# Adding the down projection's partial sums with a ScalarE copy and an accumulating DMA

## The reference, cut to what matters

```
h = rms_norm(x, pre_mlp_g)                         # x: 256 x 2048
m = jnp.square(jax.nn.relu(h @ w_up)) @ w_down     # w_up 2048 x 8192, w_down 8192 x 2048
x = x + rms_norm(m, post_mlp_g)
```

## Time and profile before

| what | value |
|---|---|
| time, two runs | 1110.64 and 1111.97 us, median 1111.31 us |
| profiled execution: span from its first to its last instruction | 1107.5 us |
| what lies around the span, by the faster run and by the median | 3.1 and 3.8 us |
| PE busy | 1091.9 us, 99% of the span |
| DVE, ACT, POOL busy | 666.2, 511.5, 98.3 us |
| DMA | 205.29 MB, mean 185 GB/s |

### The profile page before, as it was taken

The page is one execution under the profiler, slowest core; times in us unless marked ns, Lnnn a source line. Parts: engine busy times, 40 slices in busy tenths (PEclk is TensorE's granted clock), DMA queues, the critical chain, the costliest instruction groups (busy, mean ns, idle before and its releaser), DMA issues.

```text
span 1107.5 us, 13660 instructions
## 1 busy us (share of the span) xinstructions
PE 1091.9 (99%) x5034; PEld 906.2 (82%) x5034; DVE 666.2 (60%) x706; ACT 511.5 (46%) x653; POOL 98.3 (9%) x108
## 2 busy tenths in 40 slices
PE   8999999999999999999999999999999999999996
PEld 7888888887888778888888888888888888888884
DVE  5445564657985675565565655656556556565566
ACT  5564444544544464444444444444444444444443
POOL 0010120120000350000000000000000000000004
PEclk9999999999999999999999999999999999999998
DMA  9475454464755556565665655656656556566552
GB/s 330 159 227 158 155 176 138 152 196 138 274 190 191 157 185 190 189 191 160 214 190 186 197 178 192 195 159 210 189 184 200 179 189 195 166 202 193 190 172 76
DMA packets 104048, 205.29 MB, mean 185 GB/s; under 512 B 3536, under 2 KB 9552, under 8 KB 103504
## 3 DMA queue, kind: packets, MB, share of 16 engines
q1 hardware_dynamic: 104016, 204.86, 57.7%
HBM read 202.74 MB, written 2.10 MB: 185 GB/s over the span
## 4 chain that ended last, share of the span: by engine, by line
PE 95%; DVE 2%; ACT 1%; POOL 1%; issue 1%; DMA 0%; SPq 0%; DVEq 0%; POOLq 0%; ACTq 0%
PE ps L566 30%; PE ps L568 30%; PE ps L567 30%; PE ps L574 3%; DVE w_lo L1113 1%; PE ps L763 1%; PE ps L761 1%; DMA x_in<-in_x 0%; PE ps L811 0%; DVE xT_lo L1310 0%; ACT a_sb L1075 0%; ACT u_sb L939 0%; DVE acc L1339 0%; DVE x_res L1155 0%; DVE acc L1330 0%
## 5 line engine op out<-in xcount | busy, mean ns | idle before, releaser
L1113 DVE TENSOR_TENSOR w_lo<-raw,w_hi 128x1024 fp32r<-128x1024 f32 (+1 forms) x384 | 472.2, 1237 | 389.5 <-ACT w_hi L860 389.1
L860 ACT ACTIVATE w_hi<-raw 128x1024 fp32r<-128x1024 f32 (+1 forms) x384 | 398.1, 1039 | 492.7 <-PE ps L568 487.7
L566 PE MATMUL ps<-w_hi,xT_hi 128*128 128x512 f32 (+1 forms) x800 | 315.8, 395 | 1.9 <-DVE xT_lo L1125 0.7
L568 PE MATMUL ps<-w_lo,xT_hi 128*128 128x512 f32 (+1 forms) x800 | 310.0, 387 | 0.0
L567 PE MATMUL ps<-w_hi,xT_lo 128*128 128x512 f32 (+1 forms) x800 | 309.5, 387 | 0.0
L566 PE MATMUL ps<-w_hi,yT_hi 128*128 128x512 f32 x672 | 263.1, 392 | 0.0
L568 PE MATMUL ps<-w_lo,yT_hi 128*128 128x512 f32 x672 | 261.7, 389 | 0.0
L567 PE MATMUL ps<-w_hi,yT_lo 128*128 128x512 f32 x672 | 261.5, 389 | 0.0
L566 PEld LDWEIGHTS ps<-w_hi,xT_hi 128*128 128x128 f32 x800 | 150.5, 188 | 34.3 <-issue 5.6
L568 PEld LDWEIGHTS ps<-w_lo,xT_hi 128*128 128x128 f32 x800 | 150.4, 188 | 30.7
L567 PEld LDWEIGHTS ps<-w_hi,xT_lo 128*128 128x128 f32 x800 | 150.7, 188 | 27.9
(11 more groups left out here) (143 smaller groups left out, 459.8 us busy)
## 6 DMA issues: line engine op xcount, KB each, us to landing
raw<-in_w_up SPq DMA_DIRECT2D x64, 1024.0 KB, 5.3
raw<-in_w_down SPq DMA_DIRECT2D x64, 1024.0 KB, 5.0
raw<-in_w_in SPq DMA_DIRECT2D x31, 1024.0 KB, 5.2
raw<-in_w_o SPq DMA_DIRECT2D x16, 1024.0 KB, 5.1
raw<-in_w_uq SPq DMA_DIRECT2D x8, 576.0 KB, 4.0
raw<-in_w_ukv SPq DMA_DIRECT2D x4, 1024.0 KB, 5.0
raw<-in_w_in SPq DMA_DIRECT2D x4, 640.0 KB, 4.1
x_res<-in_x SPq DMA_DIRECT2D x1, 2048.0 KB, 9.2
```

The costliest lines, as they stand in the source:

```text
L566: nc.tensor.matmul(dst, x_hi, hi, start=first, stop=False)
L568: mm = nc.tensor.matmul(dst, x_hi, lo, start=False, stop=last)
L860: nc.scalar.activation(w_hi[:, slot, 0:size], raw[:, raw_slot, first:first + size], ACT.Copy).then_inc(hi_ready, 1)
L1113: nc.vector.tensor_tensor(w_lo[:, slot, 0:size], raw[:, raw_slot, first:first + size], f32(w_hi[:, slot, 0:size]), ALU.subtract).then_inc( ...
```

## The change

`add_down` leaves DVE. In its place ACT copies the finished PSUM pair into a new SBUF buffer `stage`, which has two places (quads even and odd), and POOL issues a DMA that adds that place to the columns of `acc` (`accum_op=ALU.add`). This holds for the 62 adds of a whole quad; the four block adds of `m_add` (1330) stay on DVE. Three semaphores take the place of `acc_added`: `acc_staged` (a copy is done, and PE may reuse the banks), `acc_landed[0]` and `acc_landed[1]` (a DMA of an even or odd quad has landed, 16 each), `acc_zeroed` (POOL's own memsets).

```diff
+            def stage_down(i, done, copies, landed):
+                act.wait_ge(half_used, done)
+                if landed is not None:
+                    act.wait_ge(acc_landed[i % 2], landed)
+                bank = 4 + 2 * (i % 2)
+                nc.scalar.activation(stage[:, i % 2], ps[:, bank:bank + 2], ACT.Copy).then_inc(acc_staged, 1)
...
+                elif what == "add":
+                    stage_down(a % 4, 2 * b + 2, a, 16 * (a // 2) if a >= 2 else None)
                 elif what == "m_square":
-                    act.wait_ge(acc_added, 4 * FF_STRIPS + a - 1)
+                    act.wait_ge(acc_landed[a], 16 * ((4 * (FF_STRIPS - 1) + a) // 2 + 1))
...
+                    if i >= 8 and i % 2:
+                        q = (i - 9) // 2
+                        stage_down(q, base + (i + 1), None, 32 * (j - 1) + 16 * (q // 2))
...
-            def add_down(i, done, added):
-                dve.wait_ge(half_used, done)
-                dve.wait_ge(acc_added, added)
-                m = acc[:, :, i * W:(i + 1) * W]
-                bank = 4 + 2 * (i % 2)
-                nc.vector.tensor_tensor(m, m, ps[:, bank:bank + 2], ALU.add).then_inc(acc_added, 1)
...
                     if i == 0:
                         dve.wait_ge(g_mlp_landed, 16)
-                        dve.wait_ge(acc_added, 4 * FF_STRIPS)
+                        for i_last in range(2):
+                            dve.wait_ge(acc_landed[i_last], 16 * (2 * FF_STRIPS - 1))
...
+            def add_down(i, copies):
+                pool.wait_ge(acc_staged, copies)
+                cols = slice(i * W, (i + 1) * W)
+                nc.gpsimd.dma_start(acc[:, :, cols], stage[:, i % 2], accum_op=ALU.add).then_inc(acc_landed[i % 2], 16)
...
-            with pool.Fori(LOOP.start, LOOP.stop) as j:
+            for j in LOOP:
                 square(j)
+                for q in range(4):
+                    add_down(q, (j - 1) * 4 + (q + 1))
```

More of the change, by code:

```diff
@@ L334, in hybrid_block @@
         gained = tensor(ctx, "gained", [P, TB, W])
+        stage = tensor(ctx, "stage", [P, 2, TB, W])
         ps = ctx.enter_context(nc.psum_tensor("ps", [P, 8, W], F32))
@@ L383, in hybrid_block @@
         aT_filled, aT_hi_ready, aT_lo_ready = sem("aT_filled"), sem("aT_hi_ready"), sem("aT_lo_ready")
-        acc_added = sem("acc_added")
+        acc_zeroed, acc_staged = sem("acc_zeroed"), sem("acc_staged")
+        acc_landed = [sem("acc_landed0"), sem("acc_landed1")]
         m_gained_pool = sem("m_gained_pool")
@@ L663, in stream @@
                         pe.wait_ge(aT_lo_ready, z["j"] + 1)
-                        pe.wait_ge(acc_added, 4 * z["j"] + z["q"] + 1)
+                        if 4 * z["j"] + z["q"] >= 2:
+                            pe.wait_ge(acc_staged, 4 * z["j"] + z["q"] - 1)
                         if z["j"] == 0:
@@ L694, in down_quad @@
             def down_quad(i, half, added):
-                pe.wait_ge(acc_added, added)
+                pe.wait_ge(acc_staged, added)
                 for k in range(4):
@@ L845, in _ @@
                 for i in range(4):
-                    down_quad(i, base + (8 + 2 * i), (j - 1) * 4 + (i + 1))
+                    down_quad(i, base + (8 + 2 * i), (j - 1) * 4 + (i - 1))
                 hidden_transposes(j)
@@ L1316, in step @@
                     hidden_lo(a, b)
-                elif what == "add":
-                    add_down(a % 4, 2 * b + 2, a + 2)
                 elif what.startswith("m_add"):
@@ L1355, in _ @@
                 for i in range(16):
-                    if i >= 8 and i % 2:
-                        add_down((i - 9) // 2, base + (i + 1), (j - 1) * 4 + ((i - 9) // 2 + 2))
                     split_lo(i % AHEAD, (i + AHEAD) // 2 % RAW, (i % 2) * 2 * W, 2 * W,
@@ L1482, in step @@
                     for tb in range(TB):
-                        nc.gpsimd.memset(acc[:, tb], 0.0).then_inc(acc_added, 1)
+                        nc.gpsimd.memset(acc[:, tb], 0.0).then_inc(acc_zeroed, 1)
+                    pool.wait_ge(acc_zeroed, TB)
                 elif what == "x2" and a >= X2_DVE:
@@ L1498, in step @@
                     square(a)
+                elif what == "add":
+                    add_down(a % 4, a + 1)
                 elif what == "m_square":
```

## The result

| | before | changed |
|---|---|---|
| time, two runs each | median 1111.31 us | 1117.72 and 1116.85, median 1117.28 us |
| ratio, 95% interval | | 1.0068, 1.0051 to 1.0084 |
| span of the profiled execution | 1107.5 us | 1115.8 us |
| busy DVE, ACT, POOL | 666.2, 511.5, 98.3 us | 596.2, 568.1, 172.5 us |

The time rose by 6.0 us, the span by 8.3 us; the forecast was +9.05. The changed kernel run again later, beside the kernel before on one chip, gave 1118.38 us against 1109.80 us, ratio 1.0080 (1.0066 to 1.0093).

A forecast was written before the change was run, and what follows sets the result against it. PE was taken to bound the loop, other engines' order the end. No loop cost; the end's sum, 2 D - 2.95 us, with D = 6.0 gives +9.05 us: span 1116.55, time 1120.4 us, range 1114 to 1130.5.

The forecast's parts named there:

- D: Time from a copy's end to its DMA's landing, POOL's issue included; estimated 6.0 us, bounds 3.2 and 11.1.
- Loop at no cost: In the strips, ACT copies, POOL issues and DMA traffic were to be hidden behind dense PE: cost 0.
- Copy 1.10 us: ACT's copy of a 128x1024 PSUM pair, taken as 1.10 us, four per strip.
- the slow DMAs: Rival: loop unharmed, D between 8 and 11.1 at the end, +13 to +19 us, 1124.4 to 1130.5; chance 0.13.
- Landing of quad 0 at 1087.46: At the end, strip 15: copy starts 1080.36, ends 1081.46, and its DMA lands at 1087.46.
- Landing of quad 1 at 1097.40: At the end: POOL, free at 1091.40 after its multiplies, issues quad 1's DMA, which lands at 1097.40.
- DVE's first block add waits for both DMAs: +8.40 us: At the end: DVE's first block add starts at 1097.40 instead of 1089.00.
- PE's stall of 2.4 us, at no cost: At the end: quad 3's second half is split late, moving PE's last matmul to about 1099, before DVE wants it.
- Span +9.05: Sum at the end: +8.40 us on DVE's block add and +0.65 us on ACT's squares, span 1116.55.
- the forecast's own case: D between 4.5 and 8, giving 1117.4 to 1124.4 us; chance 0.55.
- the quick DMA: Rival: D between 3.2 and 4.5 at the end, +3.4 to +6 us, 1114.7 to 1117.4; chance 0.20.
- The full engines: Rival: accumulating DMAs fill the 16 engines, loop weight loads come late; over 2% from 5.2 us per DMA; chance 0.11.

The follow-up runs named there:

- copies alone: The changed kernel without the 62 DMAs and the waits for them, ScalarE's copies kept, whole-quad adding left out: 1110.45 us, ratio 1.0001.
- sixty DMAs: The changed kernel with strip 15's two adds back on VectorE from PSUM, the 60 others still copies and accumulating DMAs: 1110.03 us, ratio 1.0001.
- with two DMAs: The changed kernel with a second accumulating DMA of the same staged copy into a spare buffer behind each of the 62: 1126.13 us, ratio 1.0152.
- with three: The kernel with two accumulating DMAs per add, plus a third of the same copy into a buffer no longer used: 1264.77 us, ratio 1.1387.
- The relaxed kernel: The changed kernel, but VectorE's first block add waits only for the DMAs up to strip 14: 1118.25 us, ratio 1.0072.
- a move of one line: The changed kernel with squares and multiplies of columns 0 moved behind quad 1's copy and DMA: 1113.88 us, ratio 1.0038.

## Why the prediction was right

The mechanism and the place were right, and each step can be held against the traces. The size of one term, D, was hit partly by luck.

- *Loop at no cost.* Shown: transposes 0.17 us apart after 14 strips, copies alone 1.0001, sixty DMAs 1.0001. The cover held with room: landings in the changed kernel came 8.5 us after the issue in the median and 11.2 at most (0.3 us more from the copy's end), under the 14.5 us from the copy's end at which I expected PE to stall. That threshold was reckoned too low: with two DMAs the last landing came up to 15.3 us after its issue and 16.3 after the copy, and PE was still dense; with three the median was 18.4 from the issue, and PE stalled.
- *Copy 1.10 us.* 1.03.
- *D = 6.0 for quad 0.* From the end of the copy, 1081.92, to the landing, 1087.95: 6.03, made of 1.04 before POOL's issue starts (0.30 in the loop) and 4.99 from issue to landing. The parts are not those of my sum. I added 1.0 for POOL's issue to a row of 5.0 that counts from the start of the issue; the measured 4.99 holds POOL's issue of 1.19 already. What filled the sum up to 6.03 was a delay before the issue that I had not in it: the total of D is right by luck in this part. Both ends of my range were far off, so the slow DMAs fall as well; the 1024 KB row was the right neighbour, and a plain DMA of 512 KB would have taken 3.12 us.
- *Landing of quad 0 at 1087.46.* 1087.95, since the copy began 0.53 us later: 0.17 of shift, and the rest a wait for the DMA of strip 14 that stood on the same place and had run beside other transfers.
- *Landing of quad 1 at 1097.40.* 1096.83. Here the term was too large: the copy had long ended when POOL came free, and from POOL's issue it is 4.96, not 6.0. The 1.0 too much outweighs the 0.5 us by which the first landing was late.
- *"DVE's first block add waits for both DMAs: +8.40 us"* puts the shift on the wrong wait. The relaxed kernel shows that. Between landing and end the chain goes over ACT's squares of columns 1 and then POOL's multiplies of 2.96 us, which hold POOL's first step of the reciprocal root. The shift is the same since all of them wait for the one landing; from the start of the block add to the end of the chain it took 15.0 us against the 15.3 of the sum. No run takes POOL's multiplies out of the way, so that they and not ACT's square of the block set the end is read from the chain only.
- *PE's stall of 2.4 us, at no cost.* Two gaps of 1.70 and 1.10 us in front of quad 3. Only the second waits for the split that I named; the first waits for the copy of quad 1, which I had not in the sum. The last matmul ended at 1100.15 instead of 1096.65, before VectorE's last block add at 1106.10. Harmless, as said.
- *Span +9.05.* +8.13 behind the loop, +8.3 in all; by the ratios +7.3 to +9.3 us in time. The missing 0.9 us is 0.6 of the second landing and 0.3 behind the block add. The first two runs (1117.28 us) lie just under the forecast's own case of 1117.4 to 1124.4, the later ones (1118.38) in it.

Of the rivals, the quick DMA (D of 3.2 to 4.5) was what a plain one does, 3.12 us from its issue; the price of adding excluded it, which was argued beforehand and is now measured. The Trainium skill's rule that an add in the DMA runs at half the rate (Collectives: The Full Stack, The bandwidth ceiling) agrees with 2.6 against 1.2 us of the engines. Its fit for a DMA issued by GpSimd (DMA: Bandwidth & Descriptors, Anatomy of one DMA) gives, as an estimate, 3.2 us for a plain 512 KB, and 3.12 were measured; with the rate halved its estimate is 4.4, against 4.96 measured, of which 0.46 is the longer issue. The full engines were a real danger, but my threshold for them was set too low: I took a share of 1 as full, and at 1.05 no strip was longer.

Open: why POOL started quad 0's issue 1.04 us after the copy and not 0.30, as in 59 of the 62. It does so again in the second trace; with plain DMAs it is 1.78 us, with only the last two adds by DMA 0.62. Open is also at which traffic between two and three DMAs per add the loop tips.

## What to carry to other kernels

An engine that is idle half the time while PE is dense gives nothing when it is relieved; look instead for the stage where the work that is moved will be waited for. Moving an add to a DMA turns a 1.2 us step into one of about 6 us; that is free where the result is needed much later and the DMA engines have room, and is paid once for each link where the next steps hang on it (here 8 us for two): keep the last adds of an accumulation on a compute engine. Before two such waits end up in a row, look at what stands between them in the order of the issuing engine: a move of one line gave back half of the loss here.

## What the runs showed of the hardware

- An accumulating DMA of 512 KB in SBUF takes the 16 DMA engines 2.6 us, a plain one 1.2 (by the rise of the share in the loop; 2.9 and 1.3 by the queue's own line); alone they land 4.96 and 3.12 us after the issue, and occupy POOL for 1.19 and 0.73 us.
- The sum of packet times can be over 1.0 of 16 engines (1.05 with two DMAs per add) with no strip longer; with three it is 1.06 by the same view, and strips are 53.3 us long. So a share just over 1 does not tell traffic that is just borne from traffic that is too high. The landing times still grow: loads of `w_up` and `w_down` land in 5.3 and 5.0 us before, 9.0 and 12.5 with two, 12.8 and 16.8 with three.
- The bytes by which the page counts an accumulating DMA are those of one source: 32.51 MB for 62, the same as for the plain ones. If the destination is read too, GB/s understates what is read.
